# Two transformer blocks in one program: next weight split, gated residual, spatial mixing and query stage in a new order

## The chip, the cores and the metric

The kernel runs on one NeuronCore of one Trainium2 chip. The time is device microseconds of one execution; before the change three timed runs gave 1240.09, 1241.09 and 1241.26 us, median 1241.09. The engines are TensorE (PE, matmuls), VectorE (DVE), ScalarE (ACT), GpSimd (POOL) and SyncE (SP, which issues the large DMAs).

## The reference

Batch 1, 256 tokens, width 1024, all in float32. Block one: adaptive norm from `silu(c) @ w_ada`, then latent attention and a two-way retention side by side on x and a context of 256 tokens, then a convolutional FFN, then a norm. Block two has two layers, cut here to what matters:

```python
# layer 0
y = gmlp_mixer(modulate(rms_norm(x, pre_mix_g[0]), sh, sc))   # z = gelu(h @ w_in + b); u, v = split(z)
                                                              # v = layer_norm(v) ; ws = tril(w_s)
                                                              # y = (u * (ws @ v + b_s)) @ w_out
x = x + g_m * rms_norm(y, post_mix_g[0])
x = x + g_f * rms_norm(swiglu(modulate(rms_norm(x, pre_ffn_g[0]), ...)), post_ffn_g[0])
k, v, dcum = shared_kv(x)          # k rms-normed per head, dcum = cumsum(log_sigmoid(f)) per head
# layer 1
q, gate = split(h @ w_qg); q = rms_norm(q) per head (16 heads of 64)
p = softmax(q k^T / 8 + dcum[t] - dcum[s], causal)
y = (p v * sigmoid(gate)) @ w_o    # then the same residual and the same FFN as in layer 0
```

## The kernel before

**Weights.** All matrices are cut into 161 units of 128 x 2048 numbers. SP loads a unit into one of four `raw` buffers (`send`, L2505 on). ACT copies it in a rounded format into `wh` (`hi_part`, L1226), DVE forms the rest `raw - wh` in `wl` (`lo_part`, L569, called by `take`, L645), and PE multiplies three times (high x high, high x low, low x high; `three`, L1721). `wh` and `wl` have two buffers each, so the split of unit u waits for the matmuls of u-2 (`w_used`), and PE waits for `lo_done`. `front_low` and `front_high` do a unit in two halves.

**Order.** Every engine runs a list written by hand; engines meet only in semaphores. `take(u)` also appends, after the split, steps of the modulation sums (`ada_part`, L577): the product `silu(c) @ ada_w` is summed on DVE in `acc` over eight steps of 128 rows, in ten groups of 2048 columns. The table `ADA_AFTER` says behind which unit a step stands. PE sums `acc` over partitions (`column_products`, one-column matmuls put between those of a unit; `extract_gate`, full rows), DVE takes the results (`extract`), and then POOL clears `acc` and loads the next bias (`start_acc`, L2377).

**Boundaries.** After each output product (`last_product`) comes `both_rows` (the residual of two row tiles, with an rms norm of the product in the second block, `residual`, L709) and `next_rows` (norm of the new x, PE turns it with `turn`, ACT and DVE evacuate it in four pairs as high and low parts, `evac_high`, `evac_low`). On DVE and ACT the split of unit `then` stands between the second and third pair. `row_root` (L1263) takes the root from two partial sums: the first, scaled, is the bias of the root ("beta").

**gMLP (L1021 on).** Four quarters of v are projected, biased and passed through gelu; then DVE takes all eight `bn_stats`, the norm, four quarters of scale and shift (L1050), and after them four masked spatial matrices `wst` (L1057). PE runs `partners(0)`, `partners(1)` (the u half) and then `spatial(0)`, which waits for all four masks and all eight affine steps.

**Queries (L1088 on, ACT L1637, PE L2264).** Units 107 to 115 are keys, values and forget logits, 116 to 123 queries and gates, 124 to 127 the output. After unit 121 and before 122 PE turns all heads of the keys (`turn_heads`, eight quads of two heads through four PSUM banks; ACT and DVE copy alternate quads), after 123 those of the queries; then 16 heads of attention (`fox_scores`, `fox_turn`, `fox_values`). Group 8 of the sums ends behind unit 114 and goes out in unit 118, and group 9 begins behind 118.

## Time and profile before

| what | value |
|---|---|
| median of three runs | 1241.09 us |
| the profiled execution | 1250.33 us, of which span 1248.5 us |
| PE busy | 1154.1 us (92%) |
| PE weight loads | 996.3 us (80%), beside PE |
| DVE busy | 841.0 us (67%) |
| ACT busy | 598.1 us (48%) |
| POOL busy | 249.9 us (20%) |
| mean granted PE clock | 0.972 |
| DMA | 263.43 MB, mean 211 GB/s |

Busy times are of the profiled execution and overlap each other. A line of a timeline gives start, length, engine, source line, operation, what it writes and reads, how many were merged, and in brackets the idle time of the engine ahead of it with what ended that. `L1723` to `L1725` are the three matmuls of `three`, so their tile names tell the place. A granted clock of 1.00 is 2.4 GHz, 0.50 is 1.2 GHz.

### The profile page before, as it was taken

How to read it: one execution, taken by the hardware profiler on the slowest of the kernel's cores; microseconds unless marked ns; L12 is line 12 of the kernel's file. 1: busy time of each engine (PE TensorE's matmuls, PEld its weight loads, DVE VectorE, ACT ScalarE, POOL GpSimd, SP SyncE). 2: the span in 40 equal slices, each digit the busy share in tenths (PEclk: the TensorE clock that was granted, in tenths of full speed). 3: DMA queues.
4: the chain of work that ended last, by engine and by line, in shares of the span. 5: the costliest groups of instructions: out<-in, count | busy, mean ns of one | idle time of the engine just before them, and what ended most of it. 6: DMA issues, size and time to landing. Idle time of an engine off the chain costs nothing.

```text
span 1248.5 us, 18186 instructions
## 1 busy us (share of the span) xinstructions
PE 1154.1 (92%) x7032; PEld 996.3 (80%) x7032; DVE 841.0 (67%) x873; ACT 598.1 (48%) x862; POOL 249.9 (20%) x168
## 2 busy tenths in 40 slices
PE   5899899989999989979979999998878898999997
PEld 1677658879999767879879999777656786999986
DVE  3795754778887868787666757657938757444444
ACT  4662455366555345434454444245515647444433
POOL 1026500015665120010012323000202000222300
PEclk9999999999999999999999999898989989999999
DMA  9776810348786987766548797955837404556450
GB/s 333 293 269 208 321 68 1 103 142 285 242 299 221 361 269 243 262 203 237 169 152 289 249 335 256 351 186 181 285 130 282 135 1 136 168 171 199 175 197 34
DMA packets 124303, 263.43 MB, mean 211 GB/s; under 512 B 8297, under 2 KB 76465, under 8 KB 114001
## 3 DMA queue, kind: packets, MB, share of 16 engines
q1 hardware_dynamic: 121553, 254.56, 58.3%
q0 software_dynamic: 2688, 8.02, 2.2%
q8 instruction: 42, 0.69, 0.2%
q14 instruction: 20, 0.16, 0.0%
HBM read 261.50 MB, written 1.05 MB: 210 GB/s over the span
## 4 chain that ended last, share of the span: by engine, by line
PE 66%; DVE 17%; issue 7%; ACT 6%; DMA 2%; SPq 1%; DVEq 0%; POOL 0%; ACTq 0%
PE ps L1723 19%; PE ps L1725 18%; PE ps L1724 18%; DVE acc L586 4%; DVE wl L574 3%; ACT wh L1236 2%; DMA raw<-in_w_in_dram 2%; DVE x L723 1%; PE ps L2014 1%; PE ps L2000 1%; PE ps L2030 1%; PE ps L1758 1%; DVE xn L721 1%; DVE hraw L700 1%; DVE acc L664 1%
## 5 line engine op out<-in xcount | busy, mean ns | idle before, releaser
L574 DVE TENSOR_TENSOR wl<-raw,wh 128x2048 fp32r<-128x2048 f32 (+1 forms) x154 | 356.4, 2315 | 248.5 <-ACT wh L1236 248.2
L1236 ACT ACTIVATE wh<-raw 128x2048 fp32r<-128x2048 f32 (+1 forms) x154 | 291.8, 1895 | 369.8 <-PE ps L1725 369.0
L1723 PE MATMUL ps<-hh,wh 128*128 128x256 f32 (+1 forms) x1192 | 340.7, 286 | 14.6 <-DVE hl L706 9.3
L1724 PE MATMUL ps<-hl,wh 128*128 128x256 f32 (+1 forms) x1192 | 337.0, 283 | 0.0
L1725 PE MATMUL ps<-hh,wl 128*128 128x256 f32 (+1 forms) x1192 | 336.9, 283 | 0.0
L1723 PEld LDWEIGHTS ps<-hh,wh 128*128 128x128 f32 (+1 forms) x1192 | 226.1, 190 | 18.2 <-DVE hl L706 6.9
L1724 PEld LDWEIGHTS ps<-hl,wh 128*128 128x128 f32 (+1 forms) x1192 | 226.2, 190 | 0.2
L1725 PEld LDWEIGHTS ps<-hh,wl 128*128 128x128 f32 (+1 forms) x1192 | 226.1, 190 | 0.2
L2460 POOL TENSOR_TENSOR gl<-hid,gh 128x256 f32 (+1 forms) x66 | 101.3, 1534 | 322.0 <-ACT gh L1564 322.0
L1723 PE MATMUL ps<-wh,hh 128*128 128x512 f32 (+1 forms) x352 | 141.7, 402 | 19.4 <-DVE wl L574 9.9
L586 DVE SCALAR_TENSOR_TENSOR acc<-au,cs,acc 128x2048 f32<-128x2048 f32 x56 | 143.1, 2556 | 16.6 <-DMA acc<-in_ada_b_dram 14.9
L1724 PE MATMUL ps<-wl,hh 128*128 128x512 f32 (+1 forms) x352 | 138.8, 394 | 0.0
L1725 PE MATMUL ps<-wh,hl 128*128 128x512 f32 (+1 forms) x352 | 138.4, 393 | 0.0
L1723 PE MATMUL ps<-wh,gh 128*128 128x512 f32 x264 | 106.7, 404 | 1.8 <-DVE acc L586 1.2
L1725 PE MATMUL ps<-wh,gl 128*128 128x512 f32 x264 | 105.8, 401 | 0.0
L1724 PE MATMUL ps<-wl,gh 128*128 128x512 f32 x264 | 105.7, 400 | 0.0
L1723 PEld LDWEIGHTS ps<-wh,hh 128*128 128x128 f32 x352 | 68.6, 195 | 39.3 <-DVE wl L574 12.1
L1725 PEld LDWEIGHTS ps<-wh,hl 128*128 128x128 f32 x352 | 68.4, 194 | 15.3
L1724 PEld LDWEIGHTS ps<-wl,hh 128*128 128x128 f32 x352 | 68.5, 195 | 13.9
L2383 POOL MEMSET acc<- 128x2048 f32 x9 | 16.6, 1849 | 269.7 <-PE ps L1853 232.5
L2457 POOL TENSOR_TENSOR hid<-sl,hu 128x256 f32<-128x256 f32 x22 | 54.2, 2465 | 55.6 <-ACT sl L1555 55.6
L1723 PEld LDWEIGHTS ps<-wh,gh 128*128 128x128 f32 x264 | 50.5, 191 | 14.4 <-issue 2.6
(319 smaller groups left out, 1509.1 us busy)
## 6 DMA issues: line engine op xcount, KB each, us to landing
au<-in_ada_w_dram SPq DMA_DIRECT2D x48, 1024.0 KB, 7.1
raw<-in_ffn_w_gu_dram SPq DMA_DIRECT2D x88, 512.0 KB, 4.7
raw<-in_w_up_dram SPq DMA_DIRECT2D x44, 512.0 KB, 4.8
raw<-in_ffn_w_down_dram SPq DMA_DIRECT2D x44, 512.0 KB, 4.3
au<-in_w_ada_dram SPq DMA_DIRECT2D x18, 1024.0 KB, 5.4
raw<-in_a_w_in_dram SPq DMA_DIRECT2D x32, 512.0 KB, 4.9
raw<-in_w_down_dram SPq DMA_DIRECT2D x22, 512.0 KB, 4.8
raw<-in_w_in_dram SPq DMA_DIRECT2D x16, 512.0 KB, 4.8
```

What stands on the lines that cost most here:

```text
L574: nc.vector.tensor_tensor(wl[:, s % 2, 0:n], raw[:, u % RAW, 0:n], wh[:, s % 2, 0:n].bitcast(F32), ALU.subtract).then_inc(lo_done, 1)
L586: nc.vector.scalar_tensor_tensor(acc[:, :], au[:, v % 2, :], cs[:, at:at + 1], acc[:, :], ALU.mult, ALU.add).then_inc(acc_step, 1)
L664: nc.vector.scalar_tensor_tensor(acc[:, :], au[:, j, :], cs[:, bass.ds(16 + j + 2 * i, 1)], acc[:, :], ALU.mult, ALU.add).then_inc(acc_ste ...
L700: nc.vector.tensor_scalar(hraw[:, 1, at:at + TOK], ps[:, TURN_BANKS[n][2 * (j // 2) + 1], at:at + TOK], mod[:, n, 0, k:k + 1], mod[:, n, 1 ...
L721: link(nc.vector.scalar_tensor_tensor(xn[:, t, cc], acc_t, rs_of(r, t), gate[:, slot, cc], ALU.mult, ALU.mult))
L1236: nc.scalar.activation(wh[:, s % 2, 0:n], raw[:, u % RAW, 0:n], ACT.Copy).then_inc(hi_done, 1)
L1723: nc.tensor.matmul(to, lh, rh, start=start, stop=False, skip_group_check=True)
L1724: nc.tensor.matmul(to, lh, rl, start=False, stop=False, skip_group_check=True)
L1725: return nc.tensor.matmul(to, ll, rh, start=False, stop=stop, skip_group_check=True)
L2383: nc.gpsimd.memset(acc[:, :], 0.0).then_inc(acc_zeroed, 1)
L2457: nc.gpsimd.tensor_tensor(hid[:, c, :], sl[:, c, :], hu[:, c, 0, :], ALU.mult).then_inc(hid_pool, 1)
L2460: nc.gpsimd.tensor_tensor(gl[:, at_, :], hid[:, c:c + 1, :], gh[:, at_, :].bitcast(F32), ALU.subtract)\
```

## The change

It moves work; nothing of what is computed changes.

- `next_rows`: ACT splits unit `then` in two halves right after the root; DVE splits the first half before the first evacuation and the second half after two pairs.
- The second block's residual takes the gate product before the root, and multiplies by the reciprocal root in the step that adds to x. The beta step runs between the two squares.
- gMLP: `bn_stats` of a quarter stand in the wait for the next one; masks are made per quarter, and each spatial product waits for its own quarter.
- Group 7's columns go into unit 103 instead of 102, group 8's steps stand behind 106 to 116 and its columns in unit 117, group 9's first step behind 119 and its last two behind 126 and 127.
- Queries: the forget unit is split between two pairs; the head sums of keys stand behind unit 116; keys are turned in two portions, before and after unit 122; scores wait quad by quad and use other banks first; the split of 125 moves behind the attention; the first half of the output is turned a head earlier.

```diff
@@ line 141 @@
 _spread(7, range(95, 103))
-_spread(8, [105, 106, 109, 110, 111, 112, 113, 114])
-_spread(9, [118, 119, 120, 121, 122, 123, 124, 127])
-EXTRACT_AFTER = {7: 1, 104: 7}
+_spread(8, [106, 109, 110, 111, 112, 113, 114, 116])
+_spread(9, [119, 120, 121, 122, 123, 124, 126, 127])
+EXTRACT_AFTER = {7: 1, 105: 7}
@@ line 311 @@
         q_st = in_r("q_st", 48, [P, NT, D])
-        qa = in_h("qa", 0, [P, NT, FH, FA])
+        qa = [in_h("qa0", 8.25, [P, FH, FA]), in_r("qa1", 40, [P, FH, FA])]
@@ line 341 @@
         SCORE_BANKS = (4, 5, 2, 3)
-        FOX_BANKS = (4, 5, 2, 3, 4, 5, 2, 3, 4, 5, 4, 5, 4, 5, 4, 5)
+        FOX_BANKS = (2, 3, 4, 5, 2, 3, 4, 5, 4, 5, 4, 5, 4, 5, 4, 5)
@@ line 642 @@
+            def front_first(u):
+                s = split_no(u)
+                fronts[0] += 1
+                dve.wait_ge(hi_first, fronts[0])
+                nc.vector.tensor_tensor(wl[:, s % 2, 0:D], raw[:, u % RAW, 0:D], wh[:, s % 2, 0:D].bitcast(F32),
+                                        ALU.subtract)
+            def front_second(u):
+                s = split_no(u)
+                dve.wait_ge(hi_done, s + 1)
+                nc.vector.tensor_tensor(wl[:, s % 2, D:], raw[:, u % RAW, D:], wh[:, s % 2, D:].bitcast(F32),
+                                        ALU.subtract).then_inc(lo_done, 1)
+                taken.append(("w", u))
@@ line 706 @@
-            def residual(t, parts, slot, r, ready, bank):
+            def acc_part(t, cc, bank):
+                b0 = bank + 2 * t + cc.start // HALF
+                return ps[:, b0:b0 + (cc.stop - cc.start) // HALF, :].rearrange("p a c -> p (a c)")
+            def residual(t, parts, slot, ready, bank):
                 for i, cc in enumerate(parts):
-                    if r is None:
-                        dve.wait_ge(*ready[i])
-                    elif i == 0:
-                        row_rstd(r, t)
-                    b0 = bank + 2 * t + cc.start // HALF
-                    acc_t = ps[:, b0:b0 + (cc.stop - cc.start) // HALF, :].rearrange("p a c -> p (a c)")
-                    if r is None:
-                        link(nc.vector.tensor_tensor(xn[:, t, cc], acc_t, gate[:, slot, cc], ALU.mult))
-                    else:
-                        link(nc.vector.scalar_tensor_tensor(xn[:, t, cc], acc_t, rs_of(r, t), gate[:, slot, cc],
-                                                            ALU.mult, ALU.mult))
+                    dve.wait_ge(*ready[i])
+                    link(nc.vector.tensor_tensor(xn[:, t, cc], acc_part(t, cc, bank), gate[:, slot, cc], ALU.mult))
+            def normed_residual(t, parts, slot, r, bank):
+                for i, cc in enumerate(parts):
+                    dve.wait_ge(sq_done, SQ_BASE[r] + 1 + t + i)
+                    ins = nc.vector.tensor_tensor(xn[:, t, cc], acc_part(t, cc, bank), gate[:, slot, cc], ALU.mult)
+                link(ins)
+                row_rstd(r, t)
+                for cc in parts:
+                    nc.vector.scalar_tensor_tensor(x[:, t, cc], xn[:, t, cc], rs_of(r, t), x[:, t, cc], ALU.mult,
+                                                   ALU.add).then_inc(x_ready, 1)
-                residual(0, whole, slot, r, ((acc_done, 2 * place + 1),), bank)
-                residual(1, halves, slot, r, ((acc_done, 2 * place + 2), (w_used, split_no(last_unit) + 1)), bank)
+                if r is None:
+                    residual(0, whole, slot, ((acc_done, 2 * place + 1),), bank)
+                    residual(1, halves, slot, ((acc_done, 2 * place + 2), (w_used, split_no(last_unit) + 1)), bank)
+                else:
+                    normed_residual(0, whole, slot, r, bank)
+                    normed_residual(1, halves, slot, r, bank)
@@ line 944 @@
                 normalise(r, 1, halves)
+                front_first(then)
                 evac_low(n, hl, hh, (0, 1))
-                take(then)
+                front_second(then)
@@ line 1018 @@
+            def gelu_stats(b):
+                for t in range(NT):
+                    dve.wait_ge(v_gelu, 2 * b + t + 1)
+                    ins = nc.vector.bn_stats(bns[:, t * 4 + b, :], vg[:, t, b * HALF:(b + 1) * HALF])
+                return ins
@@ line 1028 @@
                                             bc[:, b, :], ALU.add).then_inc(v_added, 1)
+                if b >= 1:
+                    gelu_stats(b - 1)
                 take(GM_V + 2 * b + 3)
-            for t in range(NT):
-                for b in range(4):
-                    dve.wait_ge(v_gelu, 2 * b + t + 1)
-                    ins = nc.vector.bn_stats(bns[:, t * 4 + b, :], vg[:, t, b * HALF:(b + 1) * HALF])
-            link(ins)
+            link(gelu_stats(3))
@@ line 1043 @@
             take(U_UNIT[1])
-            for b in range(4):
+            def affine_quarter(b):
                     dve.wait_ge(affine, j - 3)
-                if b == 0:
-                    take(U_UNIT[1] + 1)
-            for q in range(4):
-                dve.wait_ge(ws_turned, q + 1)
-                nc.vector.tensor_tensor(wst[:, 4 * q:4 * q + 4, :], ps[:, q, :].rearrange("p (g t) -> p g t", g=4),
+                dve.wait_ge(ws_turned, b + 1)
+                nc.vector.tensor_tensor(wst[:, 4 * b:4 * b + 4, :], ps[:, b, :].rearrange("p (g t) -> p g t", g=4),
                                         bcast(tri, 1, 4), ALU.mult).then_inc(wst_ready, 1)
+            affine_quarter(0)
+            affine_quarter(1)
+            take(U_UNIT[1] + 1)
+            affine_quarter(2)
+            affine_quarter(3)
@@ line 1087 @@
                 take(u)
-            evac_low(N_MIX2, hl2, hh2, range(4))
+            evac_low(N_MIX2, hl2, hh2, (0, 1))
+            take(KV + 8)
+            evac_low(N_MIX2, hl2, hh2, (2, 3))
@@ line 1104 @@
-            take(KV + 8)
+            take(QG)
             head_sums(ksq, R_KH, 0)
-            take(QG)
+            take(QG + 1)
@@ line 1115 @@
             nc.vector.memset(ka[:, :, :, FD:FD + 1], 1.0)
-            for u in range(QG + 1, QG + 4):
-                take(u)
+            take(QG + 2)
@@ line 1125 @@
             nc.vector.scalar_tensor_tensor(az, z, -1.0, z, ALU.mult, ALU.max).then_inc(f_pre, 1)
+            extract(8)
+            take(QG + 3)
@@ line 1132 @@
             nc.vector.tensor_tensor(ls, mn, ln, ALU.subtract).then_inc(ls_ready, 1)
-            extract(8)
@@ line 1141 @@
-            def turned_heads(to, base):
-                for q in range(0, 8, 2):
-                    dve.wait_ge(f_turned, base + q + 2)
-                    nc.vector.tensor_copy(to[:, 2 * q + 2:2 * q + 4, :],
-                                          ps[0:FA, 4 + (q + 1) % 4, :].rearrange("p (h t) -> p h t", h=2))\
+            def turned_heads(to, base, quads):
+                for q in quads:
+                    dve.wait_ge(f_turned, base + q + 1)
+                    nc.vector.tensor_copy(to[:, 2 * q:2 * q + 2, :],
+                                          ps[0:FA, 4 + q % 4, :].rearrange("p (h t) -> p h t", h=2))\
-            turned_heads(kt_f, 0)
+            turned_heads(kt_f, 0, (1, 3))
                 c = R_AT[R_QH] + t * FH
-                to = qa[:, t, :, 0:FD]
+                to = qa[t][:, :, 0:FD]
                 nc.vector.tensor_tensor(to, to, bcast(gq[:, 0, :], 1, FH), ALU.mult)
-            nc.vector.memset(qa[:, :, :, FD + 1:FD + 2], 1.0)
-            nc.vector.tensor_copy(qa[:, :, :, FD], dcum[:, :, :]).then_inc(qa_ready, 1)
+                nc.vector.memset(qa[t][:, :, FD + 1:FD + 2], 1.0)
+                nc.vector.tensor_copy(qa[t][:, :, FD], dcum[:, t, :]).then_inc(qa_ready, 1)
+            turned_heads(kt_f, 0, (5, 7))
             take(WO)
-            turned_heads(qt_f, 8)
-            take(WO + 1)
+            turned_heads(qt_f, 8, (1, 3, 5, 7))
@@ line 1204 @@
                     fox_gated(0, h - 9).then_inc(fo_gated, 1)
-                if h == 13:
+                if h == 12:
                 fox_gated(1, t).then_inc(xn_ready, 1)
+            take(WO + 1)
@@ line 1269 @@
                     act.wait_ge(sq_done, SQ_BASE[r] + 3)
-                    nc.scalar.activation(rt[:, c + 2:c + 3], ss[:, c + 1:c + 2], ACT.Identity, scale=1.0 / D,
-                                         bias=eps[:, :]).then_inc(beta_ready, 1)
-                    links[0] += 1
@@ line 1282 @@
                     squares(r, [src(t, cc)], junk, t + i)
+                    if t == 1 and i == 0:
+                        c = R_AT[r]
+                        act.wait_ge(sq_done, SQ_BASE[r] + 2)
+                        nc.scalar.activation(rt[:, c + 2:c + 3], ss[:, c + 1:c + 2], ACT.Identity, scale=1.0 / D,
+                                             bias=eps[:, :]).then_inc(beta_ready, 1)
+                        links[0] += 1
@@ line 1510 @@
                 x_squares(r, x_base)
-                evac_high(n, hh, (0, 1))
-                hi_part(then)
-                evac_high(n, hh, (2, 3))
+                front_high(then)
+                evac_high(n, hh, range(4))
@@ line 1667 @@
                     hi_part(WO)
+                if b == 2:
+                    root(R_QH)
@@ line 1678 @@
                 if b == 2:
-                    root(R_QH)
@@ line 2152 @@
                     pe.wait_ge(gl_done, NFF * f + 2 * j + 2 + CREDIT)
-                    acc_product(DOWN[f] + j, gh, gl, 2 * j, j == 0, False, None, 7 if f == 1 and j == 6 else None)
+                    acc_product(DOWN[f] + j, gh, gl, 2 * j, j == 0, False, None, 7 if f == 1 and j == 7 else None)
@@ line 2203 @@
-                if b == 0:
-                    pe.wait_ge(wst_ready, 4)
-                    pe.wait_ge(affine, 8)
-                else:
+                pe.wait_ge(wst_ready, b + 1)
+                pe.wait_ge(affine, 2 * b + 2)
+                if b >= 1:
@@ line 2261 @@
-            def queries_gates(b):
+            def queries_gates(b, hs=range(2)):
                 pe.wait_ge(evac, EVACS + 6 + 2 * b)
-                for h in range(2):
+                for h in hs:
                                  [ps[:, 2 * (b % 2) + t, :] for t in range(2)], 512, 4 * h, 4, h == 0, h == 1,
-                                 8 * N_MIX2, 8 if (b, h) == (1, 0) else None)
-                    if (b, h) == (1, 0):
-                        extract_gate(8)
-            def turn_heads(src, base):
-                for q in range(8):
+                                 8 * N_MIX2, 8 if (b, h) == (0, 1) else None)
+            def turn_heads(src, base, quads):
+                for q in quads:
                         h, t = 2 * q + j // 2, j % 2
-                        ins = nc.tensor.transpose(ps[0:FA, 4 + q % 4, j * P:(j + 1) * P], src[:, t, h, :], ident)
+                        ins = nc.tensor.transpose(ps[0:FA, 4 + q % 4, j * P:(j + 1) * P], src[t][:, h, :], ident)
@@ line 2287 @@
             ins.then_inc(f_cols, 1)
+            extract_gate(8)
@@ line 2298 @@
             pe.wait_ge(ex_taken, EX_BASE[9])
-            turn_heads(ka, 0)
-            queries_gates(3)
-            pe.wait_ge(qa_ready, 1)
-            turn_heads(qa, 8)
-            pe.wait_ge(ft_evac, 8)
-            pe.wait_ge(act_step, 8)
+            ka_rows = [ka[:, t] for t in range(NT)]
+            turn_heads(ka_rows, 0, range(4))
+            queries_gates(3, (0,))
+            turn_heads(ka_rows, 0, range(4, 8))
+            queries_gates(3, (1,))
+            pe.wait_ge(qa_ready, NT)
+            turn_heads(qa, 8, range(8))
@@ line 2311 @@
                     pe.wait_ge(fp_ready, 2 * held[-1] + 2)
+                q = h // 2
+                if h % 2 == 0:
+                    pe.wait_ge(ft_evac if q % 2 else act_step, 4 + q // 2 + 1)
+                if h == 2:
+                    pe.wait_ge(act_step, 7)
+                if h == 3:
+                    pe.wait_ge(ft_evac, 7)
@@ line 2321 @@
                 pe.wait_ge(fp_ready, 2 * h + 2)
+                if h < 2:
+                    pe.wait_ge(ft_evac if h else act_step, 8)
@@ line 2348 @@
                     fox_values(h - 1)
-                if h == 12:
+                if h == 11:
```

## Rows read from the trace of the kernel before

**Rows 1.** The page, chain that ended last, by engine.
```profile
PE 66%; DVE 17%; issue 7%; ACT 6%; DMA 2%; SPq 1%; DVEq 0%; POOL 0%; ACTq 0%
```
**Rows 2.** Windows: length, busy per engine (instructions), granted clock, DMA share, GB/s.
```profile
268.00:272.00 4.00, 4.00 (x23) 4.00 (x22) 2.23 (x1) 1.02 (x2) 0.00 (x0) 0.57 0.21 59
531.00:537.00 6.00, 5.49 (x46) 5.52 (x47) 5.93 (x5) 1.76 (x1) 1.07 (x2) 1.00 0.75 249
642.00:648.00 6.00, 5.33 (x32) 5.33 (x33) 3.03 (x4) 3.63 (x4) 0.00 (x0) 0.72 0.48 146
802.00:818.00 16.00, 15.95 (x58) 13.87 (x59) 2.29 (x1) 1.09 (x2) 2.33 (x2) 0.57 0.52 190
915.00:924.00 9.00, 9.00 (x48) 7.25 (x47) 0.00 (x0) 4.17 (x4) 0.00 (x0) 1.00 0.37 118
...
1012.00:1020.00 8.00, 7.86 (x33) 7.30 (x34) 4.52 (x9) 2.94 (x10) 0.00 (x0) 0.57 0.00 0
```
**Rows 3.** Timelines (PE, DVE) at the boundary to layer 0's FFN, first FFN unit 74.
```profile
642.67 0.39 PE L1723 MATMUL ps<-hh,wh 128*128 128x256 f32 x1 [2.09 <-DVE hl L706]
637.60 2.29 DVE L574 TENSOR_TENSOR wl<-raw,wh 128x2048 fp32r<-128x2048 f32 x1 [1.38 <-ACT wh L1236]
623.73 1.28 DVE L721 SCALAR_TENSOR_TENSOR xn<-ps,rs,gate 128x1024 f32<-128x1024 f32 x1
```
**Rows 4.** Timeline of ACT at the boundary to the gMLP.
```profile
467.57 0.56 ACT L1323 ACTIVATE hraw<-ps,mod 128x256 f32<-128x256 f32 x1 [1.50 <-PE ps L1748]
```
**Rows 5.** Timelines of the gMLP: DVE, ACT, PE.
```profile
520.51 4.84 DVE L1035 BATCH_NORM_STATS2 bns<-vg 128x6 f32<-128x512 f32 x8
543.43 2.49 DVE L1050 TENSOR_TENSOR vg<-vg,bc 128x1024 f32<-128x1024 f32 x2 [2.43 <-DMA bc<-in_a_ln_g_dram]
545.95 2.48 DVE L1057 TENSOR_TENSOR wst<-ps,con 128x512 f32<-128x512 f32 x4
545.02 1.55 ACT L1609 ACTIVATE ub<-ps,col 128x256 f32<-128x256 f32 x4
531.51 0.36 PE L1723 MATMUL ps<-hh,wh 128*128 128x256 f32 x1 [2.16 <-DVE wl L574]
548.49 3.46 PE L2214 MATMUL ps<-wst,vg 128*128 128x128 f32 x16 [5.39 <-DVE wst L1057]
```
**Rows 6.** Timelines (PE, ACT) of layer 0's output product, units 102 and on.
```profile
802.05 0.48 PE L1723 MATMUL ps<-wh,gh 128*128 128x512 f32 x1 [1.15 <-DVE acc L586]
817.81 1.92 ACT L1236 ACTIVATE wh<-raw 128x2048 fp32r<-128x2048 f32 x1 [14.91 <-PE ps L1725]
823.46 1.92 ACT L1236 ACTIVATE wh<-raw 128x2048 fp32r<-128x2048 f32 x1 [3.73 <-PE ps L1725]
```
**Rows 7.** Timelines of the query stage: PE, DVE, ACT.
```profile
898.10 0.28 PE L1723 MATMUL ps<-hh,wh 128*16 128x256 f32 x1 [1.08 <-DVE wl L574]
934.08 0.79 PE L1723 MATMUL ps<-wh,hh 128*128 128x512 f32 x1 [8.75 <-DVE wl L574]
961.21 3.52 PE L2281 MATMUL ps<-con,ka 128*66 128x128 f32 x16 [4.74 <-ACT kt_f L1659]
986.27 0.55 PE L2327 MATMUL ps<-con,prob_f 128*128 128x128 f32 x3 [1.08 <-ACT prob_f L1699]
897.87 2.47 DVE L1097 TENSOR_REDUCE ss<-ksq 128x16 f32<-128x1024 f32 x2
929.47 2.35 DVE L586 SCALAR_TENSOR_TENSOR acc<-au,cs,acc 128x2048 f32<-128x2048 f32 x1 [14.91 <-DMA acc<-in_ada_b_dram]
901.67 1.91 ACT L1236 ACTIVATE wh<-raw 128x2048 fp32r<-128x2048 f32 x1
```
**Rows 8.** Timelines of the attention tail and output: PE, DVE, ACT.
```profile
1012.14 0.82 PE L2327 MATMUL ps<-con,prob_f 128*128 128x128 f32 x3 [1.47 <-ACT prob_f L1699]
1032.45 2.29 DVE L574 TENSOR_TENSOR wl<-raw,wh 128x2048 fp32r<-128x2048 f32 x1 [1.38 <-ACT wh L1236]
1035.97 1.06 ACT L1245 ACTIVATE wh<-raw 128x1024 fp32r<-128x1024 f32 x1 [2.04 <-PE ps L1725]
```

## The prediction

> **What bounds the kernel now.** I read the chain of waits by engine first [rows 1]: TensorE (PE) holds 66% of the span, VectorE (DVE) 17%. The program is one long row of weight units, each a DMA, a high half split off by ScalarE (ACT, `hi_part`), a low half by DVE (`lo_part`), then one unit of matmuls. In steady stages a unit takes PE 5.65 us (817.81 to 823.46 [rows 6]), ACT 1.9 and DVE 2.3 [rows 3], so PE sets the pace and only its stalls are to be had. Next I listed every PE instruction with idle time before it: 54 stalls of 0.25 us or more, 86 us in all. Those that the diff touches are rows 3 to 8. Third came the granted clock [rows 2]. Twelve stretches before the end run at half speed (1.2 GHz, not 2.4). The reader is to see where: behind a stall of 2.09 us (window 642 to 648, mean 0.72), behind one of 1.15 us with one-column products between the matmuls (802 to 818, mean 0.57, the longest), behind 1.47 us (1012 to 1020, 0.57); yet not behind a stall of 2.16 us (531 to 537, 1.00), nor in a unit with one-column products and no stall ahead (915 to 924, 1.00). A lost clock costs the stretch times one minus the mean: 6 x 0.28 = 1.7 us, 16 x 0.43 = 6.9, 8 x 0.43 = 3.4. So a stall is worth its length and often 1.7 us or more on top.
>
> **Part 1, the next unit's split in the boundary wait (five boundaries).** Now DVE evacuates two pairs, splits the next unit (2.29 us), evacuates two more, and PE, done with its first unit, stalls 2.09 us for the last low rows [rows 3]. In the changed order DVE splits the first half (about 1.15) while PE turns the rows, the other half between the pairs; ACT does both its halves (2 us) right after the root. Before the three FFNs DVE has 1.15 us less to do behind the turn, PE's first unit (5.9 us) outlasts it, and the 2.1 us stall goes. The half ahead of the evacuation makes DVE begin it later, by 0.8 us at the first FFN and 0.4 at the others; since DVE waited 0.3 us for ACT there anyway, PE starts 0.4 and 0.1 us later. Sum 1.7 + 2.0 + 2.0 = 5.7. The third unit's split then needs the first unit's buffer, freed 2 us earlier too, so nothing is late next. The three half-speed stretches behind these stalls (1.7 each, [rows 2]: 268 and 642, the third alike) should go: 5.1. Bounds 0 and 5.1; I take 5.1, since the stall is the only thing that precedes them.
> At the gMLP boundary PE has no stall at its second unit, so nothing is won. ACT waited only 1.50 us before its evacuation [rows 4], less than the 2 us now put there: 0.4 us lost. At the keys' boundary the same, but part 2 wins 0.8, net +0.4. Together 0.
>
> **Part 2, gate product ahead of the root, beta early.** The product takes 1.28 us with the scale in it [rows 3], as does the new final step; the same four passes per row stay. Only the start moves: to the end of the squares instead of the root and reciprocal, 0.3 us. The beta step leaves the path between squares and root (0.33 us) only where ACT had been waiting for x, the keys' boundary; before the FFNs DVE's gate extraction (1.3 us) ends later than the root. At the end of the kernel 0.3 is kept. Bounds 0 and 0.6 each.
>
> **Part 3, gMLP.** The eight statistics (4.84 us in one block [rows 5]) become two per block inside the wait for weights, so six of them, 3.6 us, leave the path. What is late next: PE's second partner unit, which stalled 2.16 us for DVE's split, also needs the banks that ACT frees 1.6 us after the first partner units end; 0.5 us is won there, not 3.1. Then DVE does 2 affine steps (1.24 each) and one mask product (0.62) per quarter. Bias rows are asked for on GpSimd as each affine step ends, 3 us earlier, so the 2.43 us DMA wait at 543.43 goes, and quarter 0 is ready near 531 instead of 548.4. PE runs from its partner units, ending near 542.7, into the spatial product without the 5.39 us stall. That product took 3.46 us for 16 passes at half speed, 1.8 at full (the later three took that). Next late: the banks ACT evacuates at 545.02 [rows 5] (1.55 us); PE goes on at 546.4 against 551.9: 5.4 won. A new stall of 1.9 us may cost a clock loss of 1.7; I charge half: 4.6. Bounds 2.0 (loss, and DVE late with unit 61, which now stands behind two quarters) and 6.
>
> **Part 4, group 7 one unit later.** PE waited 1.15 us at 802.05 for the last `ada_part` [rows 6]; one unit later the sum is 5.6 us old. The columns still go between matmuls. The unit took 15.8 us (802.05 to 817.81): 5.6, plus 16 columns (about 3.7), plus 6.5 to 6.9 of clock. Columns without a stall kept full clock in 915 to 924 [rows 2], in a unit of group 8. So 1.15 + 6.9 = 8.0; bounds 1.15 and 8.0, and I take the upper, nearest to that row.
>
> **Part 5, query stage.** Replayed on the old time axis. Unit 115's split comes between pairs: its 1.08 us stall goes, 116 starts at 901.5 not 902.85. But DVE now does 116 (2.3), a group-8 `ada_part` (2.35) and only then the head sums (2.47, at 897.87 before [rows 7]); ACT's key root waits for them, and behind it in ACT's queue stand two evacuations and the split of 117 (901.67 before). So 117's low half is ready at 911.9 (910.3 before): a new stall of 3 to 4.8 us, almost surely with a clock loss, in a unit that now holds group 8's columns. Unit 117 and the gate sums end at 923.3, or 926.6 if the columns hold the clock down as at 802; before, 118 as well was through by 925.3. From there the order pays: the gate's sums, the clearing of `acc` and its bias DMA end 4.15 us later (929.47 [rows 7]), and nothing but group 9's first step waits for them: units 118 and 119 run meanwhile, where PE stalled 8.75 us. Then keys are turned in two portions between 121, 122 and 123, whose copies lie under a unit each, so the 4.74 us stall before 961.21 goes. Queries wait for the second half of DVE's queue (the split and `ada_part` of 124, 4.6 us, stand ahead of its copies), 5 us of small stalls. Without the split of 125 ahead of the maxima, and with scores started early, the first turn of probabilities comes at 973.4 to 976.7 against 986.27: 9.6 to 12.9. Minus a possible further clock loss I take 10; bounds 4 and 15.
>
> **Part 6, attention tail.** Turning the first half a head earlier lets ACT run its evacuation without blocking the exponential behind it: 1.1 of 1.47 us [rows 8]. The clock loss behind it (3.4) I count half: 2.8 in all; bounds 0 and 4.9.
>
> **Part 7, group 9's last steps at 126 and 127.** The step at 126 (2.34) stands ahead of the last evacuation, so 127's split starts at 1034.8, not 1032.45, and ends at 1037.1; PE wanted it at 1035.9 [rows 8]. Loss 1.2, and DVE is still splitting when the squares are ready, 0.2 more, with a chance of a clock loss (0.6): -2.0; bounds -3.4 and 0. The split of 125 behind the last gate product is free, PE has 5.6 us of unit 124.
>
> **Sum.** 5.7 + 5.1 + 0 + 4.6 + 8.0 + 10 + 2.8 - 2.0 + 0.3 = 34.5 us. Against the profiled execution, 1250.3 (span 1248.5 and 1.8 around it), that gives 1215.8. That execution is 9.2 us over the median of the runs, 1241.1; I carry the difference over: 1206.6, forecast 1207.
>
> The Trainium skill ("TensorE: Matmul & The Clock Gate", The HAM clock gate) says that the activity check runs freely, not in step with the kernel, so that the same kernel changes clock at different points. That speaks against booking each lost stretch as won. The trace agrees: 2.16 us cost nothing, 1.15 us much.
>
> **Rivals.** (a) The half-speed stretches stay or move elsewhere, as those three stalls allow: minus 5.1, 6.9 and 1.7 = 20.8 won, 1220. For it: some stalls of 1 to 2 us remain in every stage; against: none stands where the long one did. (b) The query stage gives 3, because the root that now waits behind unit 116 and its clock loss eat the rest, or qa is late: 27.5 won, 1214. (c) Slower: small matmuls hold the clock down. In 802 to 818 it did not rise while one-column products were between. If the 5 us of small stalls ahead of the scores drop it and the attention heads (1.78 us each, 16 of them) never lift it, they cost up to 28 us more; with (a)'s losses, 20.8 - 28 = 7 slower, 1248. Against it: the same kind of stalls at 979 to 986 left the heads at full clock, and behind 1012 it rose within the tail. It decides if over 11 of 16 heads run slow with (a). (d) All stalls and losses go: 43 won, 1198.
>
> **Numbers.** Forecast 0.5 (own range 1201 to 1212), (a) 0.22, (b) 0.15, (c) 0.05, (d) 0.08. Range 1199 to 1223 takes (a) and (b) with some 3 us of room. A difference of 0.2% (2.5 us) is what runs of this kernel can tell: faster 0.93, within 0.02, slower 0.05.
>
> **What would show it.** Right: no stall over 0.5 us at the second unit of each FFN; clock 1.00 over the unit of group 7, which lasts 9.3 us; first spatial product right behind its partner units, 1.8 us long; no 8.75 us stall, but a new one of 3 to 5 us before unit 117; 1.2 us before unit 127. Wrong if group 7's unit still runs at half speed, or the new stall before 117 is above 7 us.

## The result, and the profile after

The changed kernel took 1210.98 us at the median, against 1241.17 for the kernel before on the same chip: ratio 0.9742, 95% interval 0.9694 to 0.9789. The forecast was 1207.0, 3.98 us too low, inside its range. Its four runs were 1212.02 (the profiled one), 1209.94, 1209.89 and one of 1233.49, which the ratio leaves out as a slow run; that last one turned out to be the most instructive number of this study.

The page of the profile after has a span of 1210.1 us (1248.5 before), mean granted clock 0.985 (0.972). First the chain that ended last, by engine [rows 1]: PE holds more of it, since it stands still less.

```profile
PE 69%; DVE 18%; issue 7%; ACT 5%; DMA 1%; DVEq 0%; POOL 0%; SPq 0%; ACTq 0%
```

Then lines of PE's timeline at the places of the change: instructions with idle time before them (and the first spatial product, L2256, that has none now). `L1766` is here the first matmul of `three`.

```profile
538.05 1.95 PE L2256 MATMUL ps<-wst,vg 128*128 128x128 f32 x16
541.73 0.39 PE L1766 MATMUL ps<-hh,wh 128*128 128x256 f32 x1 [1.73 <-ACT ub L1651]
625.11 0.36 PE L1766 MATMUL ps<-hh,wh 128*128 128x256 f32 x1 [1.35 <-DVE hl L722]
824.14 1.09 PE L1791 MATMUL ps<-con,xn 128*128 128x128 f32 x4 [5.10 <-DVE xn L704]
879.11 0.66 PE L1766 MATMUL ps<-wh,hh 128*128 128x512 f32 x1 [1.82 <-issue]
889.28 0.67 PE L1766 MATMUL ps<-wh,hh 128*128 128x512 f32 x1 [2.79 <-DVE wl L574]
946.50 0.63 PE L2321 MATMUL ps<-con,qa 128*66 128x128 f32 x4 [1.27 <-ACT qt_f L1701]
949.39 1.50 PE L2321 MATMUL ps<-con,qa 128*66 128x128 f32 x12 [2.26 <-DVE qt_f L1187]
1000.14 0.48 PE L1766 MATMUL ps<-wh,hh 128*128 128x512 f32 x1 [1.28 <-DVE wl L574]
```

A stall is idle time of PE ahead of an instruction. The stalls at the second unit of the three FFNs [rows 3] are gone; 625.11 is the first unit's wait for the rows, which stays. No wait stands before the spatial product, where 5.39 us stood [rows 5], none at group 7's unit [rows 6], and the 8.75 and 4.74 us of the query stage [rows 7] are gone too. New are 1.73 us behind the first spatial product, 2.79 before unit 117 and 1.28 before unit 127; inside the turn of the queries 1.27 and 2.26 us stand now, where the kernel before has 1.70 and 0.32. All stalls of 0.25 us and more come to 62.0 us (86.2 before).

The windows that answer to [rows 2]:

```profile
531.00:545.00 14.00, 12.27 (x104) 12.08 (x104) 13.83 (x12) 5.29 (x6) 2.15 (x4) 1.00 0.74 246
626.00:634.00 8.00, 8.00 (x69) 8.00 (x68) 5.42 (x10) 5.86 (x9) 0.00 (x0) 1.00 0.43 133
792.00:812.00 20.00, 20.00 (x105) 16.85 (x104) 6.84 (x5) 7.24 (x5) 2.33 (x2) 1.00 0.54 186
888.00:900.00 12.00, 10.72 (x34) 9.14 (x35) 6.05 (x6) 0.94 (x1) 0.00 (x0) 0.57 0.54 175
948.00:988.00 40.00, 38.30 (x279) 35.61 (x280) 27.18 (x63) 22.99 (x81) 0.00 (x0) 1.00 0.15 52
1014.00:1020.00 6.00, 4.69 (x27) 4.70 (x27) 5.64 (x12) 4.21 (x10) 0.00 (x0) 0.72 0.07 15
```

Group 7's unit (in 792 to 812) has full clock, unit 117 (888 to 900) half, layer 1's FFN boundary a short fall though no second-unit stall is left. Summing length times one minus the clock over windows of 2 us gives 19.8 us lost (35.5 before). So of the 38.4 us between the two spans 24.2 are stalls and 15.7 clock, with 1.5 the other way.

By stage, from turn to turn: to the gMLP's turn 210.9 to 206.8 us, to layer 0's FFN 165.4 to 158.6, to the keys' turn 214.9 to 203.2, to the first turn of probabilities 140.5 to 129.2, to layer 1's FFN 60.9 to 57.9, to the end 201.3 to 198.9.

### The profile page after: what moved, and what is told of

Read it like the earlier page. It is cut to its first block, busy times and chain, and to the rows that moved or that the text cites. A ratio compares the mean times of both kernels' runs of the same rounds, so it can differ in the third digit from the quotient of the medians.

```text
span 1210.1 us, 18225 instructions
## 1 busy us (share of the span) xinstructions
PE 1139.8 (94%) x7032; PEld 983.6 (81%) x7032; DVE 839.9 (69%) x880; ACT 597.1 (49%) x866; POOL 250.2 (21%) x168
## 4 chain that ended last, share of the span: by engine, by line
PE 69%; DVE 18%; issue 7%; ACT 5%; DMA 1%; DVEq 0%; POOL 0%; SPq 0%; ACTq 0%
PE ps L1766 20%; PE ps L1768 19%; PE ps L1767 19%; DVE acc L586 5%; DVE wl L574 3%; ACT wh L1276 2%; PE ps L2057 1%; PE ps L2043 1%; PE ps L2073 1%; DMA au<-in_w_ada_dram 1%; PE ps L1801 1%; DVE acc L680 1%; DVE hu L995 1%; DVE x L745 1%; DVE xn L741 1%
## 5 line engine op out<-in xcount | busy, mean ns | idle before, releaser
L574 DVE TENSOR_TENSOR wl<-raw,wh 128x2048 fp32r<-128x2048 f32 (+2 forms) x149 | 343.2, 2304 | 237.8 <-ACT wh L1276 237.5
L1276 ACT ACTIVATE wh<-raw 128x2048 fp32r<-128x2048 f32 (+2 forms) x149 | 282.4, 1895 | 362.6 <-PE ps L1768 362.4
L1766 PE MATMUL ps<-hh,wh 128*128 128x256 f32 (+1 forms) x1192 | 339.2, 285 | 8.8 <-DVE hl L722 4.0
L1766 PEld LDWEIGHTS ps<-hh,wh 128*128 128x128 f32 (+1 forms) x1192 | 224.7, 188 | 11.7 <-issue 5.7
L1766 PE MATMUL ps<-wh,hh 128*128 128x512 f32 (+1 forms) x352 | 141.5, 402 | 15.0 <-DVE wl L574 5.0
L1768 PE MATMUL ps<-wh,hl 128*128 128x512 f32 (+1 forms) x352 | 137.9, 392 | 0.0
L1766 PE MATMUL ps<-wh,gh 128*128 128x512 f32 x264 | 104.8, 397 | 0.6 <-DVE wl L574 0.6
L1766 PEld LDWEIGHTS ps<-wh,hh 128*128 128x128 f32 x352 | 67.8, 193 | 35.1 <-issue 10.4
L1766 PEld LDWEIGHTS ps<-wh,gh 128*128 128x128 f32 x264 | 49.5, 188 | 12.7 <-issue 1.0
```

The costliest lines, as they stand in the source:

```text
L574: nc.vector.tensor_tensor(wl[:, s % 2, 0:n], raw[:, u % RAW, 0:n], wh[:, s % 2, 0:n].bitcast(F32), ALU.subtract).then_inc(lo_done, 1)
L1276: nc.scalar.activation(wh[:, s % 2, 0:n], raw[:, u % RAW, 0:n], ACT.Copy).then_inc(hi_done, 1)
L1766: nc.tensor.matmul(to, lh, rh, start=start, stop=False, skip_group_check=True)
L1768: return nc.tensor.matmul(to, ll, rh, start=False, stop=stop, skip_group_check=True)
```

## The experiments

Twelve experiments on three chips, e1 to e4, e5 to e8 and e9 to e12; the kernel before had medians of 1241.62, 1241.84 and 1241.86 beside them. All are compared with the changed kernel (1210.98), where nothing else is said.

| run | median us (lowest, highest) | lost to the clock in its profile |
|---|---|---|
| e1 front undone | 1222.67 (1219.3, 1241.53) | 28.6 |
| e2 group 7 undone | 1217.62 (1214.64, 1232.57) | 23.1 |
| e3 query stage undone | 1219.91 (1218.57, 1224.65) | 21.4 |
| e4 sums first | 1225.66 (1225.24, 1226.26) | 36.6 |
| e5 heads clear | 1208.46 (1206.58, 1209.69) | 21.8 |
| e6 both | 1200.13 (1197.24, 1204.52) | 19.5 |
| e7 changed again | 1234.26 (1212.49, 1237.24) | 45.0 |
| e8 gMLP undone | 1239.4 (1235.88, 1241.28) | 51.9 |
| e9 before again | 1241.45 (1239.76, 1265.05) | 25.1 |
| e10 e6, gMLP undone | 1206.15 (1205.37, 1209.88) | 18.2 |
| e11 e6, part 2 undone | 1203.34 (1202.44, 1205.22) | 18.2 |
| e12 e6 again | 1201.90 (1199.84, 1211.63) | 16.8 |

**e1, part 1 undone.**

```diff
-                front_first(then)
                 evac_low(n, hl, hh, (0, 1))
-                front_second(then)
+                take(then)
```

(ScalarE alike: `evac_high`, `hi_part(then)`, `evac_high`.)

> The changed kernel (1210.98) with one part undone: at the five boundaries ScalarE and VectorE again split the next unit between two pairs of evacuations, as the kernel before did. Prediction's step: a stall of 2 us at the second unit of each FFN comes back (5.7 together) and a half-speed stretch behind each (1.7 each, 5.1 together), so 10.8 slower, 1221.8. Rival, from the profile after, where a half-speed stretch stands in 1014 to 1020 though no stall does at the second unit: the stretches aren't bound to these stalls, and only 5.7 and at most the two other stretches come back: 5.7 to 9.1, 1216.7 to 1220.1. Second rival: the stall was hidden anyway (the first unit of the FFN waits for the same rows), under 2 slower.

Measured 11.7 slower. PE's timeline has the stalls at the first two FFNs again, and the windows show what stands behind them:

```profile
268.18 0.39 PE L1766 MATMUL ps<-hh,wh 128*128 128x256 f32 x1 [2.09 <-DVE hl L722]
637.91 0.39 PE L1766 MATMUL ps<-hh,wh 128*128 128x256 f32 x1 [2.09 <-DVE hl L722]
266.00:274.00 8.00, 5.91 (x50) 5.82 (x50) 5.68 (x10) 4.42 (x7) 0.00 (x0) 1.00 0.50 156
636.00:644.00 8.00, 6.09 (x38) 6.09 (x39) 4.44 (x6) 4.79 (x7) 0.00 (x0) 0.79 0.54 166
```

The same 2.09 us stall cost no clock at one place and 1.7 us (8 x 0.21) at the other. At layer 1's FFN the clock was already low from 1024 to 1030, ahead of that place, and the stall there is only 0.34. So the number of the prediction's step is met, its tie of one stretch to each stall is not. By stage, e1's profile is 12.9 us longer than the one after: 3.4 up to the gMLP's turn, 3.4 between layer 0's FFN and the keys' turn, 0.8 behind layer 1's FFN turn, which makes 7.6 where the FFN boundaries are; 3.6 fall in the query stage (a stall of 4.33 before unit 117 and a longer stretch behind it, for one) and 1.7 in the gMLP's, mostly as clock.

**e2, part 4 undone:** the columns in unit 102 again.

```diff
-EXTRACT_AFTER = {7: 1, 105: 7}
+EXTRACT_AFTER = {7: 1, 104: 7}
-  ... 7 if f == 1 and j == 7 else None)
+  ... 7 if f == 1 and j == 6 else None)
```

> The changed kernel with group 7's one-column products and extraction back in unit 102, one unit earlier. Prediction's step: the 1.15 us stall and the half-speed stretch of 16 us (6.9 lost) come back, 8.0 slower, 1219.0, granted clock near 0.57 over some 15 us behind the stall. Rival: the long stretch was that execution's own (its profile was 9.2 us over the median of the runs, and the other terms were not): then only the stall comes back, 1.2 slower, 1212.1, with the clock at 1.00 or a short dip of 2 to 4 us.

The stall came back to the hundredth; the clock did not fall:

```profile
790.36 0.47 PE L1766 MATMUL ps<-wh,gh 128*128 128x512 f32 x1 [1.15 <-DVE acc L586]
790.00:800.00 10.00, 9.64 (x58) 8.56 (x59) 2.50 (x2) 1.40 (x2) 1.72 (x1) 1.00 0.82 308
```

The stage from layer 0's FFN to the keys' turn is 204.6 us against 203.2, so 1.4 there. The median is 6.6 slower all the same; this profile loses 3.3 us more to the clock than the one after, at other places (6.8 instead of 5.1 in unit 117, for one). The rival holds for the place. The median agrees with neither (8.0 and 1.2), and that it lies nearer to the 8.0 does not speak for the prediction's step, whose place has full clock.

**e3, parts 5 and 7 undone:** `_spread(8, ...)`, `_spread(9, ...)`, `qa`, `FOX_BANKS` and the query stage of all three engines as before.

> The changed kernel with the query stage, the groups 8 and 9, the early scores and the split of unit 125 as in the kernel before (parts 5 and 7 undone, the attention tail kept as changed). Prediction's steps: 10 back for the query stage and 2.0 saved at the end of attention, 8 slower, 1219. From the profiles: the stage from the turn of the keys' rows to the first turn of probabilities went from 140.5 to 129.2 us and the last stage's 1.3 us stall goes away, so 10 slower, 1221. Rival: what the stage gained is a clock difference between two executions: under 5 slower.

8.9 slower. The stalls of 8.72 and 4.74 us are back, the stage takes 137.9 us against 129.2, and the stage behind it 56.3 against 57.9, with no stall at unit 127.

**e4, the head sums ahead of group 8's last step.**

```diff
-            take(QG)
+            lo_part(QG, split_no(QG))
+            taken.append(("w", QG))
             head_sums(ksq, R_KH, 0)
+            for v in ADA_AFTER[QG]:
+                ada_part(v)
```

It follows from these rows of the changed kernel (DVE, ACT): the sums end at 883.64, the root and two evacuations stand ahead of unit 117's high half, and the low half waits for that.

```profile
878.92 2.34 DVE L586 SCALAR_TENSOR_TENSOR acc<-au,cs,acc 128x2048 f32<-128x2048 f32 x1
881.18 2.46 DVE L1136 TENSOR_REDUCE ss<-ksq 128x16 f32<-128x1024 f32 x2
886.93 2.29 DVE L574 TENSOR_TENSOR wl<-raw,wh 128x2048 fp32r<-128x2048 f32 x1 [3.07 <-ACT wh L1276]
883.90 0.23 ACT L1301 ACTIVATE rt<-ms 128x32 f32<-128x32 f32 x1 [7.22 <-DVE ms L1138]
```

> The changed kernel, but the sums of squares of the keys' heads stand ahead of group 8's last accumulation at unit 116, not behind it. In the profile after, ScalarE waits 7.2 us for them, unit 117's split follows, TensorE stalls 2.79 us and units 117 and 118 run at half speed for 12 us (5.3 lost). Theory (the stall drops the clock and group 8's one-column products hold it down): the sums come 2.34 us earlier, the stall shrinks to about 0.5, the stretch goes, 7.6 faster, 1203.4. Rival (the stretch comes from the one-column products or by chance): 2.3 faster, 1208.7. Second rival: what is won is given back ahead of the queries' turn, where TensorE waits for VectorE: within 1 us, 1211.

All of it came at its place, and still the kernel was 14.7 us slower than the changed one, where 7.6 faster was expected. PE's timeline and windows:

```profile
887.49 0.50 PE L1769 MATMUL ps<-wh,hh 128*128 128x512 f32 x1 [0.55 <-DVE wl L574]
942.88 2.35 PE L2324 MATMUL ps<-con,qa 128*66 128x128 f32 x10 [2.22 <-DVE qt_f L1190]
888.00:912.00 24.00, 24.00 (x112) 18.92 (x112) 17.42 (x19) 11.55 (x12) 3.77 (x4) 1.00 0.68 239
944.00:988.00 44.00, 44.00 (x180) 41.29 (x179) 16.05 (x41) 16.58 (x63) 0.00 (x0) 0.50 0.08 29
988.00:996.00 8.00, 7.84 (x59) 7.37 (x60) 3.83 (x10) 4.75 (x17) 0.00 (x0) 0.94 0.00 0
```

The stall before unit 117 is 0.55, the unit with the columns has full clock, and the first turn of probabilities comes 3.4 us earlier, though the scores before it already ran at half speed. Then the attention heads run at half clock to 988, with PE busy 44 of 44 us: 23.9 lost. This is rival (c) of the prediction. It also explains the changed kernel's run of 1233.49. Span times mean clock is 1191.9 and 1190.9 for the two runs of 1212.02 and 1209.94 and 1190.9 for that one: the same work, 22 us more at the lower clock. That its heads were the place was still a guess.

**e5, clear queues ahead of the heads:** on DVE and ACT nothing but copies stands before the scores.

```diff
-            take(WO)
             turned_heads(qt_f, 8, (1, 3, 5, 7))
...
+                if h == 1:
+                    take(WO)
+                if h in (3, 5, 7):
+                    ada_part(9 * 8 + (h + 7) // 2)
```

(`_spread(9, ...)` ends at 123; ACT's `hi_part(WO + 1)` goes behind head 2.)

> The changed kernel with nothing but copies in VectorE's and ScalarE's queues ahead of the scores: the split of unit 124, the last three accumulations of group 9 (77, 78, 79) and ScalarE's half of unit 125 go into the loop over the attention heads, where the profile after shows VectorE idle 1.15 us in every second head. Theory: both stalls inside the queries' turn (1.27 for ScalarE's copy, 2.26 for VectorE's) and the stall of 1.28 at unit 127 go, 4.8 faster, 1206; no run with the heads at half speed, so no run above 1215. Rival 1: the heads wait for VectorE now (four operations of 2.3 us against 1.15 idle each), 4 x 1.2 given back, 1211. Rival 2: what the heads' clock does has nothing to do with these stalls: some runs stay 20 us longer, as 1 of 4 of the changed kernel did.

**e6, e4 and e5 together.**

> Both: the keys' head sums ahead of group 8's last accumulation (as in the run before, 1225.66) and the clear queues ahead of the scores. In that run's profile the first turn of probabilities came 6 us earlier than in the changed kernel, but then all heads ran at half speed, 48 us from 940 to 988, 23.9 lost. Theory: the two stalls of 1.31 and 2.22 us among small products ahead of the heads dropped the clock, and the heads' own products, which keep TensorE busy but are short, never lifted it; without the stalls the heads run at full speed: 1225.7 - 20 - 5 = 1200. Rival: it is the moment at which the heads start that decides, or the products themselves; then the half speed stays and it is 1220.

(The 6 us in this text are 3.4 by the rows: the first turn of probabilities is at 949.93 in e4 and at 953.36 in the changed kernel.)

**e7, the changed kernel again.**

> The changed kernel as it is, once more, beside the two kernels above: 1211, and the profile again without a half-speed stretch in the heads. If what the clock loses is chance, the stretches of this profile stand elsewhere than in the first one (878 to 884, 888 to 900, 820 to 828, 462 to 468); if it follows from the stalls, they stand in the same places. Runs of 1233 (1 of 4 so far) are taken as runs with the heads at half speed: span times mean clock gave 1191 for all four.

The 1211 expected of e7 did not come. e5 and e7 ran on one chip and make a pair that agrees to 0.1 us until 944.9, with the same half-speed stretches up to there. e7, PE's timeline and windows:

```profile
944.94 2.08 PE L2321 MATMUL ps<-con,qa 128*66 128x128 f32 x16
948.33 0.63 PE L2321 MATMUL ps<-con,qa 128*66 128x128 f32 x4 [1.31 <-ACT qt_f L1701]
951.18 2.77 PE L2321 MATMUL ps<-con,qa 128*66 128x128 f32 x12 [2.23 <-DVE qt_f L1187]
944.00:948.00 4.00, 2.96 (x20) 1.98 (x18) 4.00 (x6) 3.08 (x4) 0.00 (x0) 1.00 0.18 76
948.00:952.00 4.00, 1.45 (x8) 1.09 (x9) 3.72 (x4) 1.35 (x3) 0.00 (x0) 0.76 0.61 184
952.00:988.00 36.00, 36.00 (x147) 33.58 (x146) 12.46 (x33) 13.44 (x50) 0.00 (x0) 0.50 0.10 38
```

and e5:

```profile
944.88 3.83 PE L2325 MATMUL ps<-con,qa 128*66 128x128 f32 x32
944.00:948.00 4.00, 3.94 (x32) 3.24 (x31) 3.50 (x8) 2.72 (x5) 0.00 (x0) 1.00 0.11 45
948.00:952.00 4.00, 3.85 (x28) 3.40 (x27) 3.34 (x9) 3.69 (x12) 0.00 (x0) 1.00 0.00 0
952.00:988.00 36.00, 35.41 (x249) 31.99 (x248) 30.37 (x56) 21.26 (x72) 0.00 (x0) 1.00 0.20 61
```

Up to the scores it is the same moment and the same products; only the two stalls differ, and with them 36 us of half speed. The clock fell at 950.1, inside the second stall, ahead of the heads, into which e5 moves its operations. In 952 to 988 e5 gets through 249 records, e7 through 147. The changed kernel took 1234 (1232.21 to 1237.24) in five of six runs here and 1212.49 in one; e5 took 1208.46 with none above 1209.69.

The two stalls do not always do this, and the profiles show how it parts. All six with the stalls have them within 0.04 us of each other. In the one after the clock did not fall. In e1 and e2 it fell inside the second stall too (at 959.7 and 953.1), but rose again 0.6 and 0.3 us into the scores, and the heads ran at full speed:

```profile
959.50:963.50 4.00, 3.45 (x17) 3.08 (x17) 2.42 (x4) 1.48 (x2) 0.00 (x0) 0.57 1.06 375
963.50:1000.00 36.50, 36.23 (x263) 33.60 (x263) 23.83 (x59) 21.42 (x80) 0.00 (x0) 1.00 0.03 10
```

(These are e1's; e2 has a clock of 0.51 in 953.0 to 956.5 and 1.00 behind it.) In e4, e7 and e8 the clock fell 1.1 to 1.7 us ahead of the twelve turns behind the second stall, in e1 and e2 0.3 and 0.6 us, and only in e4, e7 and e8 it stayed low through the scores. Whether this difference decides is not shown; no run moved the fall alone.

The four operations moved into the heads cost 0.43 us (one stall at 970.85), not the 4.8 of the rival: DVE's idle time there and the lookahead of two heads took them (this reason is argued, not measured). Of the 4.8 us of stalls removed, 2.5 to 4.0 show against the changed kernel's undisturbed times (1210.98, 1212.49). e6 was at 1200.13, as its theory had it. Its rows:

```profile
889.88 0.51 PE L1773 MATMUL ps<-wh,hh 128*128 128x512 f32 x1 [0.54 <-DVE wl L574]
939.04 3.83 PE L2328 MATMUL ps<-con,qa 128*66 128x128 f32 x32
886.00:898.00 12.00, 11.46 (x58) 9.07 (x57) 7.98 (x8) 4.03 (x4) 0.00 (x0) 1.00 0.70 233
936.00:980.00 44.00, 43.17 (x301) 38.46 (x300) 38.30 (x74) 25.99 (x86) 0.00 (x0) 1.00 0.20 69
```

Unit 117's stretch behaves the same way: it lost 5.1 to 6.8 us in the six profiles with a stall of 2.79 to 4.36 us before it (after, e1, e2, e5, e7, e8), and nothing in the five with the sums first (e4, e6, e10, e11, e12).

**e8, part 3 undone:** statistics, affine order and the first spatial product's wait as before.

> The changed kernel with the statistics, the scaling by quarters and the first spatial product's wait as in the kernel before. Prediction's step: the 5.39 us stall ahead of the first spatial product and 1.6 us of half speed in it come back, less what it saved at the new 1.7 us stall: 4.6 to 5.4 slower, 1216. From the profiles: the stages from the mix's turn of rows to the FFN's went from 165.4 to 158.6 us, so 6.8 with 1.7 of clock ahead of the gMLP in it: 5.1 slower. Rival: the biases' DMA or unit 61's split is late anyway: under 2 slower.

All 12 runs were near 1239, and the profile has the heads at half clock:

```profile
546.99 3.67 PE L2248 MATMUL ps<-wst,vg 128*128 128x128 f32 x16 [3.75 <-DVE wst L1085]
956.00:1004.00 48.00, 45.77 (x188) 42.87 (x188) 18.84 (x44) 17.53 (x65) 0.00 (x0) 0.51 0.14 45
```

Like against like, it is 5.1 us over e7's median, whose heads are slow too: the step holds. But everything behind the gMLP comes 7 us later, and the share of executions near 1235 and above went from five of six to twelve of twelve. The moment may have a part in it, and e10 asks which of the two decides.

**e9, the kernel before again** (no edit).

> The kernel before, once more with its profile. The prediction read twelve half-speed stretches in one profiled execution (35.5 us lost; 268 to 272, 466 to 474, 548 to 552, 642 to 648, 804 to 818, 844 to 852, 902 to 908, 930 to 938, 960 to 966, 1012 to 1020) and booked 6.9 us of group 7's unit as won. Prediction's step: the same places again, 804 to 818 among them. Rival, from the run with group 7 undone, whose 1.15 us stall was followed by full clock: the stretches move from execution to execution, group 7's unit lasts 9.3 us this time, and their sum is 5 to 10 us less, as the median of the runs lies 9.2 us under the profiled one.

The stalls are the same, 85.5 us in sum against 86.2. The clock is not: 25.1 lost against 35.5, and group 7's unit, PE's timeline and windows, had none of it:

```profile
800.33 0.47 PE L1723 MATMUL ps<-wh,gh 128*128 128x512 f32 x1 [1.15 <-DVE acc L586]
800.00:810.00 10.00, 9.67 (x59) 8.57 (x60) 2.48 (x2) 1.40 (x2) 1.75 (x1) 1.00 0.77 290
810.00:818.00 8.00, 8.00 (x36) 6.44 (x35) 3.11 (x4) 3.61 (x2) 0.59 (x2) 1.00 0.33 106
```

This execution took 1240.42, in the middle of the runs; the one that the prediction was made from took 1250.33, and the 10.4 us of clock between the two are the whole difference of the spans (9.9). The rule that the prediction cited from the Trainium skill ("TensorE: Matmul & The Clock Gate", The HAM clock gate: the activity check runs freely, so the same kernel changes clock at different points) fits that.

**e10, e6 with part 3 undone as in e8.**

> The kernel of the run of 1200.13 (sums first and clear queues ahead of the heads) with the gMLP stage undone, as in the run of 1239.4, where the changed kernel's heads ran at half speed in all 12 runs. Everything behind the gMLP comes some 7 us later than in the 1200 kernel, the queues ahead of the heads stay clear. Theory (the stalls among the small products ahead of the heads drop the clock): no run with slow heads, 1200 + 5 to 7.5, 1205 to 1208. Rival (it is the moment at which the heads start): slow heads in some or all runs, 1226 to 1230.

1206.15, no run above 1209.88, and the heads at full clock in the profile:

```profile
940.00:990.00 50.00, 49.20 (x331) 43.44 (x330) 41.89 (x77) 30.32 (x94) 0.00 (x0) 1.00 0.23 75
```

The edit that left slow heads in 12 of 12 executions with the stalls leaves 0 of 6 without them. The later moment alone does not bring them. (e8 and e10 ran on different chips; on e8's own chip the kernels without the stalls, e5 and e6, had none in 10, those with them, e7 and e8, 17 of 18.)

**e11, e6 with part 2 undone, and e12, e6 again.**

> The 1200 kernel with part 2 undone: the gate product again behind the root and the reciprocal, the beta step between squares and root. Prediction's step: 0.3 at the end and 0.8 at the keys' boundary, 1.1 slower, 1201.2; bounds 0 and 2. Rival: nothing, the two kernels within 0.5 of each other. From the profiles the stall ahead of the keys' turn went from 5.61 to 5.10.

> The kernel of the run of 1200.13 once more, on this chip: 1200, between 1197 and 1205, no run with slow heads (five of five had none). If the rival of the run beside it holds (the moment decides), one run in some is 1223.

1203.34 against 1201.90; the intervals to the kernel before overlap (0.9662 to 0.9714, 0.9653 to 0.9724), so the 1.4 is not shown by the times. The rows show it: the stall ahead of the keys' turn is 5.60 in e11 and 5.10 in e12, that ahead of layer 1's FFN 2.18 and 1.67.

```profile
1001.65 1.06 PE L1784 MATMUL ps<-con,xn 128*128 128x128 f32 x8 [2.18 <-DVE xn L704]
```

```profile
1001.65 1.06 PE L1798 MATMUL ps<-con,xn 128*128 128x128 f32 x8 [1.67 <-DVE xn L704]
```

So the best version is that of e6 and e12, 1200.1 and 1201.9 (ratios 0.9660 and 0.9689). With clear queues (e5, e6, e10, e11, e12) the highest of 28 executions was 1211.63. With the two stalls ahead of the scores, six of the changed kernel's ten were at 1232 to 1237, all sixteen of e4 and e8 at a mean clock of 0.959 to 0.971 (their two profiles have slow heads), and two of six of e1 (1241.5) and one of e2 (1232.57) some 15 to 20 over the rest: 25 of 38, where slow heads are read from times and clocks except in the three profiles that show them. Of 57 of the kernel before two were above 1260.

## Why the prediction was right or wrong

- **Part 1** (10.8 forecast): 11.7 in e1, close in number, in part by luck. The stalls went as forecast. The 5.1 of clock was booked as in part 4, a stretch of one execution taken as bound to its stall: a stretch stayed in the profile after (1014 to 1020), e1 shows that a 2.09 us stall brings one or doesn't, and only 7.6 of the 12.9 us by which e1's profile is longer stand in the stages with FFN boundaries.
- **Part 2** (0.3, and 0.8 at the keys): 0.5 us in each of two stalls (e11 against e12); the 1.4 between the medians is not clear of noise. Right at the keys, if a little less than forecast; the other 0.5 stands ahead of layer 1's FFN, where the prediction had put nothing. The 0.3 at the end was not isolated.
- **Part 3** (4.6): 5.1 by e8 against e7, 4.3 to 6.0 by e10 against e12 and e6. The new stall that was forecast at 1.9 is 1.73. The clock loss of it, charged half, did not come in the profile after; it came (1.7 us behind 541.93 and 542.96) in two of the ten profiles that have this part, e2 and e6.
- **Part 4** (8.0) is the step that failed. The 1.15 us of stall were won. The 6.9 of clock belonged to one execution: the same stall with the same columns kept full clock in e9 and in e2. The nearest row (915 to 924, full clock with columns and no stall) told that columns are harmless without a stall, and I read it as if the stall had to bring the fall.
- **Part 5** (10; bounds 4 and 15): the stage is 11.3 shorter, with 8.9 in the medians by e3, which undoes part 7 as well. The stall before unit 117 was put at 3 to 4.8 and is 2.79 here, up to 4.36 in e2; it cost its clock, as said.
- **Part 6** (2.8): with part 7 taken out, in e3, the stage is 4.6 shorter (60.9 to 56.3). The 1.47 went, and the whole 3.4 of clock, of which half was charged.
- **Part 7** (-2.0): 56.3 to 57.9, so -1.6; its stall is 1.28 against 1.2 forecast.
- **From the profile to the median.** The forecast took 34.5 off the profiled execution and then the 9.2 us by which that lay over the median. But 6.9 of the 34.5 were among those 9.2: the stretch at group 7's unit, absent in e9, is the larger part of the 10.4 us of clock that this execution lost over e9's. The same microseconds were taken off twice. Without the second count the sum gives 1213.5, 2.5 over what was measured, which parts 3, 5 and 6 being a little larger makes up. That the forecast was only 4 us off is therefore partly luck: it hides an error of 6.9 and smaller ones of the other sign. (The list of stalls behind its 86 us has 53 entries of 0.25 us and more, not 54; the sum is right.)
- **Rival (c)**, slow heads, was the one to take more seriously. It had 0.05 and a price of up to 28 us; it costs 23.9 (e4), and, by their times and mean clocks, it came in six of ten runs of the changed kernel. Of the four runs of the result one had it; in e7 five of six had, the median was 1234.26, and that lies outside the stated range (1199 to 1223). The mechanism of the rival belongs to the changed kernel, and the forecast's being in its range owes something to which runs were drawn. Even so the kernel is at 1234 then, not slower than before, since (a)'s losses, which it was coupled to, did not come with it. Its counter-argument, "the same kind of stalls at 979 to 986 left the heads at full clock", was one execution's word on a matter of chance.

What stays open: why slow heads are so much rarer in the kernel before (at most two of 57, if the two above 1260 are such; neither has a profile) and in e3 (none of 5), which have stalls of 1.70, 0.78 and 1.08 us at that place. Their longest is shorter than 2.2 us, but no run varied the length of the stall alone. Open too is why the clock came back at the first scores in e1 and e2 and not in e4, e7 and e8.

## What to carry to other kernels

Take clock losses from a profile as one draw: sum stalls and lost clock apart, compare the profiled execution's lost clock with that of the other runs (span times mean clock lay in 1187.9 to 1191.9 for the ten runs of the changed kernel, 1205 to 1215 for 53 of the kernel before), and never book a stretch as won and carry the profile's excess over as well. Rank stalls by what comes behind them: here 2 us ahead of full-width matmuls cost 2 to 4 us, 2.2 us ahead of a long row of short products cost 26 where the row stayed slow (25 of 38 executions by their times), else 2 to 4. So clear the queues of the evacuating engines before such a row, even if what is moved goes into the row itself.

## What the runs showed of the hardware

- PE was busy for 44 of 44 us at a granted clock of 0.50 (e4). The Trainium skill ("TensorE: Matmul & The Clock Gate", The HAM clock gate) has sustained matmul activity release the clock; the row of short products in the heads was unbroken and did not. In e7 the clock came back as the eight turns behind head 11 ended (1.81 us from 996.30 on, mean 0.77 in 996 to 1000), and at the same eight turns in e4 (at 989.0) and e8 (at 1004.5).
- Clock that was lost ahead of a wait for another engine cost nothing. After, e5 and e7 ran unit 116 partly at half speed and then stalled 2.79 to 2.80 us before unit 117; e1 and e2 ran 116 at full clock and stalled 4.33 and 4.36. Unit 117 began 10.17 to 10.18 us behind unit 116 either way.
- Otherwise most stalls repeat closely between executions, chips and kernels (1.15, 5.10 and 4.74 us to 0.01, 8.72 to 8.75); what varies in this kernel from run to run is nearly all clock.
